# Two-layer block: the small parameters of a layer move from SyncE's load queue to GpSimd's, and two low halves take other places on VectorE

## The reference

```python
a = rms_norm(h, attn_norm[i])
proj = a @ w_in[i]                       # 1024 x 4632 columns, split below
(da_q, da_k, da_v, ssd_z, ssd_xbc, ssd_dt,
 gla_q, gla_k, gla_v, gla_g, gla_lr) = jnp.split(proj, IN_SPLITS, axis=-1)
y_da  = diff_attention(da_q, da_k, da_v, ...)   # q, k: rms_norm by head, gain, rope
y_ssd = ssd_mixer(ssd_z, ssd_xbc, ssd_dt, ...)  # xbc: 4-tap convolution, bias, silu
y_gla = gla_mixer(gla_q, gla_k, gla_v, gla_g, gla_lr, ...)
h = h + concat(y_da, y_ssd, y_gla) @ w_out[i]
f = rms_norm(h, ffn_norm[i])
h = h + (silu(f @ w_ffn_gate[i]) * (f @ w_ffn_up[i])) @ w_ffn_down[i]
h = h + sigmoid(h @ ple_w_gate[i]) * (p[i] @ ple_w_proj[i])
```

## Time and profile before

| | |
|---|---|
| median of 3 runs | 1769.35 us (1769.14 to 1770.1) |
| the profiled execution | 1768.65 us |
| its span in the trace | 1766.5 us |
| TensorE busy with matmuls | 1709.9 us, 97% of the span |
| VectorE busy | 1202.0 us, 68% |
| ScalarE busy | 908.3 us, 51% |
| GpSimd busy | 44.2 us, 3% |
| granted TensorE clock, mean | 0.997 of full speed |

### The profile page before, as it was taken

One profiled execution on the slowest core, in us unless ns is written; L12 is line 12 of the kernel. 1 busy time (PEld: TensorE's weight loads), 2 busy tenths in 40 slices (PEclk: granted clock), 3 DMA queues, 4 the chain that ended last, 5 costly groups with the idle time before them and its releaser, 6 DMA issues.

```text
span 1766.5 us, 33950 instructions
## 1 busy us (share of the span) xinstructions
PE 1709.9 (97%) x14158; PEld 1480.2 (84%) x14158; DVE 1202.0 (68%) x1673; ACT 908.3 (51%) x1122; POOL 44.2 (3%) x47
## 2 busy tenths in 40 slices
PE   7999999998999999999999999999999989999998
PEld 5877799986987789988978888888888868899896
DVE  5888765546678865545657768678677794577874
ACT  5565443335475443334554556445454563466772
POOL 2000000000000000000000000000000000000130
PEclk9999999999999999999999999999999999999999
DMA  7657568554557566655331322222222122352112
GB/s 198 192 191 288 165 169 193 183 196 160 150 179 269 206 162 184 190 191 180 86 91 59 92 73 73 73 73 85 73 61 85 61 97 96 114 175 64 48 65 103
DMA packets 252184, 238.18 MB, mean 135 GB/s; under 512 B 32816, under 2 KB 212064, under 8 KB 251776
## 3 DMA queue, kind: packets, MB, share of 16 engines
q1 hardware_dynamic: 250896, 233.21, 42.7%
q0 software_dynamic: 1136, 2.81, 0.7%
HBM read 234.94 MB, written 1.05 MB: 134 GB/s over the span
## 4 chain that ended last, share of the span: by engine, by line
PE 82%; DVE 6%; ACT 4%; DMA 3%; DVEq 2%; issue 1%; ACTq 1%; SPq 1%
PE pg L2629 35%; PE pg L1298 34%; PE pm L1298 8%; PE pm L2629 3%; PE pm L1301 2%; DMA ring<-in_ada_w 1%; DVE ring_r L572 1%; PE pm L2632 1%; DMA ring<-in_hg_w_in 1%; DMA ring<-in_w_in 1%; ACT ring_r L565 1%; DVE ring_r L1753 1%; SPq L2218 1%; DVEq L1789 1%; DMA cst<-in_cst 0%
## 5 line engine op out<-in xcount | busy, mean ns | idle before, releaser
L572 DVE TENSOR_TENSOR ring_r<-ring,ring_r 128x2048 fp32r<-128x2048 f32 (+1 forms) x126 | 283.7, 2260 | 157.1 <-ACT ring_r L565 151.3
L2629 PE MATMUL pg<-ring_r,work_r 128*128 128x512 f32 (+1 forms) x1632 | 377.9, 391 | 7.7 <-DVEq L3138 2.7
L2629 PEld LDWEIGHTS pg<-ring_r,work_r 128*128 128x128 f32 x1632 | 299.4, 189 | 76.6 <-issue 12.6
L1298 PE MATMUL pg<-ring_r,work_r 128*128 128x512 f32 (+3 forms) x1280 | 355.8, 383 | 2.7 <-DVE work_r L1759 1.4
L2629 PE MATMUL pg<-work_r,ring_r 128*128 128x256 f32 x2688 | 320.5, 282 | 6.9 <-DVE ring_r L572 3.8
L2629 PEld LDWEIGHTS pg<-work_r,ring_r 128*128 128x128 f32 x2688 | 318.9, 189 | 8.7 <-DVE ring_r L572 5.0
L565 ACT ACTIVATE ring_r<-ring 128x2048 fp32r<-128x2048 f32 (+1 forms) x126 | 237.1, 1889 | 169.9 <-DMA ring<-in_w_ffn_up 70.2
L1298 PE MATMUL pg<-ring_r 128*128 128x512 f32 (+3 forms) x752 | 284.3, 378 | 2.5 <-DVEq L823 1.3
L1298 PEld LDWEIGHTS pg<-ring_r,work_r 128*128 128x128 f32 x1280 | 235.5, 188 | 48.1 <-issue 2.9
L1298 PE MATMUL pg<-work_r,ring_r 128*128 128x512 f32 (+1 forms) x976 | 264.6, 361 | 0.0
L1298 PEld LDWEIGHTS pg<-work_r,ring_r 128*128 128x128 f32 x976 | 173.0, 189 | 27.3
(11 more groups left out here) (395 smaller groups left out, 1854.9 us busy)
## 6 DMA issues: line engine op xcount, KB each, us to landing
ring<-in_w_in SPq DMA_DIRECT2D x36, 1024.0 KB, 5.3
ring<-in_ada_w SPq DMA_DIRECT2D x24, 1024.0 KB, 6.9
ring<-in_hg_w_in SPq DMA_DIRECT2D x48, 512.0 KB, 3.8
ring<-in_w_ffn_gate SPq DMA_DIRECT2D x44, 512.0 KB, 4.0
ring<-in_w_ffn_up SPq DMA_DIRECT2D x44, 512.0 KB, 5.3
ring<-in_w_ffn_down SPq DMA_DIRECT2D x22, 1024.0 KB, 4.9
ring<-in_hg_w_in SPq DMA_DIRECT2D x64, 256.0 KB, 3.0
ring<-in_w_out SPq DMA_DIRECT2D x12, 1024.0 KB, 5.1
```

What stands on the lines that cost most here:

```text
L572: W.low_done(V.tensor_tensor(lo, W.raw(i, name)[:, 0:lo.shape[1]], W.hi(i, name).bitcast(f32), ALU.subtract))
L1298: return T.matmul(out_, lhsT, rhs, start=first, stop=last)
L2629: return T.matmul(out_, lhsT, rhs, start=first, stop=last)
```

## The change

The list `layer_parameters` and the loop `load_parameters` become functions that GpSimd uses. SP's queue then holds only `x`, the constants and weights; it no longer waits for `dak_1`. GpSimd issues the 22 loads of layer 0 behind its three first loads, then `p`, then the five vectors of the second block. It issues the 22 loads of layer 1 in one go, behind the memset that waits for `score2` of layer 0 and behind two new waits: the normed rows of the feed-forward part (`e_aT`, 8) and the fourth finished product of gate and up (`e_gu`, 4). On VectorE the low half of `small` moves ahead of the multiplication by the gain, and the low half of `gqk_0` moves between the ropes of tile 0 and tile 1, in both layers.

```diff
@@ sync
             load_w_in(0, w_in_pieces[1:4])
-            first_loads = layer_parameters(0)
-            W.wait_ready(sp, 0, "dak_1")
-            for k, (a, b) in enumerate(((0, 12), (12, 16), (16, N_PRM))):
-                load_parameters(first_loads[a:b])
-                load_w_in(0, w_in_pieces[4 + k:5 + k])
             for i in range(DEPTH):
-                load_w_in(i, w_in_pieces[4 if i else 7:])
+                load_w_in(i, w_in_pieces[4:])
...
-                    if next_loads and j == 6:
-                        e_aT.wait(sp, i, 8)
-                    if 6 <= j < 17:
-                        load_parameters(next_loads[2 * (j - 6):2 * (j - 5)])
@@ gpsimd
-            second_pool_early(pool)
+            load_parameters(pool, layer_parameters(0))
             for i in range(DEPTH):
...
                 pool.dma_start(q3(ptok, NT), d["p"][i, 0].rearrange("(t p) n -> p t n", p=P)).then_inc(loaded_p, 16)
+                if i == 0:
+                    second_pool_early(pool)
...
                 e_zero1.set(G.memset(Sz, 0.0))
+                if i + 1 < DEPTH:
+                    e_aT.wait(pool, i, 8)
+                    e_gu.wait(pool, i, 4)
+                    load_parameters(pool, layer_parameters(i + 1))
@@ vector
                 dve.drain()
+                low("small")
                 for t in range(NT):
                     V.tensor_tensor(qk5[:, t], qk5[:, t], bc(q3(p_qkg, 2), [2, HC, DQK], 2), ALU.mult)
                 dve.drain()
-                low("small")
                 for t in range(NT):
...
                     dve.drain()
+                    if t == 0:
+                        low("gqk_0")
                 e_qk.set(dve.drain())
-                low("gqk_0")
```

More of the change, by code:

```diff
@@ L2182, in second_dve, with layer_parameters, load_parameters @@
             V.tensor_tensor(h3[:, 1, half[1]], h3[:, 1, half[1]], rows_of(1, 1), ALU.add).then_inc(m_fin, 1)
+        def layer_parameters(i):
+            small_loads = [
+                (p_convb, cols("ssd_conv_b", i)),
+                (p_qkg[:, 0:DQK], rows("da_q_norm", i)), (p_qkg[:, DQK:], rows("da_k_norm", i)),
+                (p_bgate, cols("gla_b_gate", i)), (p_wg2[0:GLA_R, :], d["gla_w_gate2"][i]),
+                (p_dtb, rows("ssd_dt_bias", i)), (p_alog, rows("ssd_a_log", i)),
+                (p_lam[:, 0:64], rows("da_lambda_q1", i)), (p_lam[:, 64:128], rows("da_lambda_k1", i)),
+                (p_lam[:, 128:192], rows("da_lambda_q2", i)), (p_lam[:, 192:256], rows("da_lambda_k2", i)),
+                (p_dskip, rows("ssd_d", i)), (p_ssdn, rows("ssd_norm", i)), (p_glan[:, 0:1], cols("gla_norm", i)),
+                (p_sub[:, 0:1], cols("da_sub_norm", i)),
+                (p_ffn, cols("ffn_norm", i)), (p_li, d["lam"][i]),
+                (p_adab, d["ada_b_2"][i].rearrange("(c p) -> p c", p=P)),
+            ]
+            for j in range(4):
+                small_loads.insert(1 + j, (convw3[:, j, :], d["ssd_conv_w"][i, j].rearrange("(c p) -> p c", p=P)))
+            assert len(small_loads) == N_PRM
+            return small_loads
+        def load_parameters(eng, loads):
+            for dst, src in loads:
+                eng.dma_start(dst, src).then_inc(loaded_prm, 16)
         @block.sync
@@ L2196, in piece @@
                     W.loaded(sp.dma_start(dst(W.raw(i, name)), src), i, name)
-            def layer_parameters(i):
-                small_loads = [
-                    (p_convb, cols("ssd_conv_b", i)),
-                    (p_qkg[:, 0:DQK], rows("da_q_norm", i)), (p_qkg[:, DQK:], rows("da_k_norm", i)),
-                    (p_bgate, cols("gla_b_gate", i)), (p_wg2[0:GLA_R, :], d["gla_w_gate2"][i]),
-                    (p_dtb, rows("ssd_dt_bias", i)), (p_alog, rows("ssd_a_log", i)),
-                    (p_lam[:, 0:64], rows("da_lambda_q1", i)), (p_lam[:, 64:128], rows("da_lambda_k1", i)),
-                    (p_lam[:, 128:192], rows("da_lambda_q2", i)), (p_lam[:, 192:256], rows("da_lambda_k2", i)),
-                    (p_dskip, rows("ssd_d", i)), (p_ssdn, rows("ssd_norm", i)), (p_glan[:, 0:1], cols("gla_norm", i)),
-                    (p_sub[:, 0:1], cols("da_sub_norm", i)),
-                    (p_ffn, cols("ffn_norm", i)), (p_li, d["lam"][i]),
-                    (p_adab, d["ada_b_2"][i].rearrange("(c p) -> p c", p=P)),
-                ]
-                for j in range(4):
-                    small_loads.insert(1 + j, (convw3[:, j, :], d["ssd_conv_w"][i, j].rearrange("(c p) -> p c", p=P)))
-                assert len(small_loads) == N_PRM
-                return small_loads
-            def load_parameters(loads):
-                for dst, src in loads:
-                    sp.dma_start(dst, src).then_inc(loaded_prm, 16)
             whole8 = lambda s: s.rearrange("p (c n) -> p c n", c=KC)
@@ L2269, in _ @@
                 wu = d["w_ffn_up"][i].rearrange("(c p) n -> p c n", p=P)
-                next_loads = layer_parameters(i + 1) if i + 1 < DEPTH else []
                 for j, name in enumerate(gu_pieces):
```

## The result

| | before | after |
|---|---|---|
| median | 1769.15 us (1766.99 to 1770.1, 16 runs) | 1772.96 us (1771.38 to 1775.61, 16 runs) |
| span of the profiled execution | 1766.5 us | 1771.1 us |
| VectorE starts the low half of `xbc1_0` | 49.68 | 54.28 |
| the 16 transposes start | 82.64 | 88.89 |

A forecast was written before the change was run, and what follows sets the result against it. TensorE holds 82% of the chain, so time can only come from its gaps and slow stretches, here at layer 0's start. 1768.65 - 5.2 = 1763.4, with 0.7 for the median 1764.1 us; range 1762.8 to 1767.

The forecast's parts named there:

- landing of `xbc0_0`: Layer 0 start: this weight piece lands at 34.5 instead of 36.27, with no SP loads around it.
- VectorE starts `xbc1_0`: Layer 0: VectorE begins this low half at 44.55 instead of 49.68, 10.05 us after `xbc0_0` lands, set by ScalarE's chain.
- chain to the end of `gqk_1`: VectorE's work from the low half of `xbc1_0` through that of `gqk_1`: unchanged 27.14 us, ending at 71.7 instead of 76.82.
- wait ahead of the second half of `gqk`: TensorE in layer 0 wants the low half of `gqk_1` at 71.05, has it at 71.7: 0.65 us wait stays.
- GpSimd's 22nd load issued by: Layer 0's 22 loads on GpSimd start at 21.50, take 17.2 us, the last issued at 38.7.
- last of the 22 landed: Layer 0's small parameters all land by 43.2; VectorE waits for them at 46.8, margin 3.6 us.
- Theory 2: From the experiments, not the prediction: small loads of any other queue in flight beside a weight piece slow it.
- Theory 1: From the experiments, not the prediction: GpSimd's queue itself is the cause, its packets hold the DMA engines.
- rival A: Layer 0 start: only issue time is saved, `xbc0_0` lands at 36.27 as before; gain 3.5, 1765.9 us; chance 15%.
- The order: VectorE's earlier low halves of `small` and `gqk_0`: costed at 0, alone also about 0.
- C: Layer 0's parameters come late from GpSimd and move VectorE's chain; at 1.5 us a load 7 us slower, 1776; chance 8%.
- B: Behind 82 us or in layer 1: the shift is given back or not taken, 1767 to 1770 us; chance 12%.

The follow-up runs named there:

- seven first on SP: Kernel before with layer 0's seven early-needed small loads ahead of four weight pieces on SP, the other 15 behind, VectorE's order of before: 1762.41 us, ratio 0.9973.
- seven first, GpSimd: Changed kernel with GpSimd issuing seven early-needed loads first, then `p`, the 15 others and five vectors after `xbc1_1` landed: 1766.68 us, ratio 0.9999.
- ScalarE's queue: Kernel before with layer 0's 22 small loads issued by ScalarE instead of SP: 1774.19 us, ratio 1.0030.
- queues alone: Changed kernel with VectorE's order of before, so only the queues of the small loads are changed: 1771.95 us, ratio 1.0021.
- last six held: Changed kernel with GpSimd's last six loads (`p`, five vectors) held back until `xbc1_1` has landed: 1769.06 us, ratio 1.0010.
- order alone: Kernel before with only the new order of low halves on VectorE: 1769.98 us, ratio 1.0005.

## Why the prediction was wrong

Each forecast number beside what the changed kernel and, where the landing was undisturbed, the best version showed:

| step | forecast | after | seven first on SP |
|---|---|---|---|
| issues of `xbc0_0`, `xbc1_0` | 28.36, 33.9 | 28.28, 33.87 | 29.09 for the first |
| landing of `xbc0_0` | **34.5** (33.71 to 36.27) | **39.7** | 35.66 |
| VectorE starts `xbc1_0` | 44.55 | 54.28 | 45.81 |
| chain to the end of `gqk_1` | 27.14 | 27.24 | 27.16 |
| wait ahead of the second half of `gqk` | 0.65 | 1.79, then half clock | 1.21 |
| GpSimd's 22nd load issued by | 38.7 | 36.3 | |
| landing of `ada_b` after its issue | 4.5 | 10.3 | |
| last of the 22 landed | 43.2 | 45.2 | |
| the kernel | -5.2 us | +3.8 us | -5.1 us |

**The step that failed** is the landing: "both ends are bounds: landing at 33.71 or at 36.27", and I took 34.5 "because behind the change there is no SP load around it and the loads that GpSimd issues at that time are short rows". The upper end was no bound: the piece landed at 39.7. It was the row of a piece beside *some* small loads; the change put more of GpSimd's beside it, and for longer. That they were "short rows" was no reason for 34.5 either: the row loads of 32 KB took four times as much packet time in GpSimd's queue as in ScalarE's (below). The steps around it were right. In the best version, with its 0.73 us taken off, `xbc0_0` lands at 34.9, VectorE starts `xbc1_0` at 45.1 and the transposes start at 78.05: a gain of 4.6 us there where the sum said 5.2, the rest being the wait of 1.21 in place of 0.65. In the medians it is 5.1 us (3.0 to 6.7 by the interval).

**Why before was better than it looked.** Two queues shared the small loads. From 18 to 28 us, while no piece was in flight, they got 13 of the 28 through; the DMA view of that window, before:

```profile
q1 hardware_dynamic: 5902, 0.13, 36.0%
q0 software_dynamic: 224, 0.03, 19.6%
```

5902 packets of SP's queue, about half of its small ones, went while TensorE worked on pieces that had landed. GpSimd alone issues a load in 0.51 to 1.43 us, 28 of them in 19.8 us: the series reaches from 21.5 to 41.3 us, over `xbc0_0`, `xbc0_1` and `xbc1_0`. I had worked this out (the last of the 22 issued at 38.7) and asked only whether the parameters would be in time, not what they would do to the pieces.

**Theory 2 holds, with a remainder.** A different queue (ScalarE's) slows the pieces too, 38.26 and 43.93 where Theory 1 had at most 36.5 and 41.5; GpSimd's loads that fly later (the last six) cost 3 us less; and with GpSimd's queue empty from 29.7 us on `xbc0_0` lands at 35.2. In SP's own queue, 15 loads *behind* a piece cost it nothing (`xbc1_1`: 45.58 - 40.26 = 5.3 us, as undisturbed). The packets in the traces say how much company there was. While `xbc0_0` was between issue and landing, packets of the other queues, and small ones of SP's own, took this much time, summed over the 16 engines:

```
                          issue to landing   other queues   SP's own small
seven first, SP                6.58 us            0 us           0 us
seven first, GpSimd            6.69               7              0
before                         7.89              17             11
ScalarE's queue                9.22              26              0
after                         11.41              81              0
queues alone                  11.77              79              0
last six held                 12.27              85              0
```

From 6.6 to 11.4 are 4.8 us on each of 16 engines, 77 us, and GpSimd's packets took 81. It is an estimate, as packets overlap, and with ScalarE's queue it comes out less well (42 against 26). It also points at why GpSimd's loads cost more than ScalarE's. They did not take more in all: from 14 to 70 us ScalarE's queue took 135.5 us for the 22, GpSimd's 173.1 with its nine others, which alone took 48.3 in the run with ScalarE's queue, so about 125. But more of it fell beside the piece. Four of the six row loads of 32 KB landed there with GpSimd (35.2 to 37.6), with ScalarE only behind it (39.3 to 43.7), and the six took 52.8 us of packet time in GpSimd's queue and 13.2 in ScalarE's. How much of the lateness is due to the time of the loads and how much to the kind of queue isn't measured.

**The rule I had cited.** The Trainium skill (DMA: Bandwidth & Descriptors, "Issuing engines are not separate DMA queues") says that loads of several engines interleave on the same 16 DMA engines. The trace agrees: from 30 to 32 us the 16 engines started 23 packets of GpSimd's queue and 270 of SP's. The other half, that issuing from more engines only saves time on the sequencer, I took in rival A to mean a landing of 36.27 as before; measured 39.7. Interleaving is not neutral: a long transfer that shares each engine with another queue lands later than one that has it to itself.

**The order** was costed at 0, "alone it would also give about 0". Its effect on waits was right (the second half of `gqk` still starts at 76.9). I had not followed the clock: when alone, the wait that moved to a place between the halves took the stretch of 1.2 GHz with it, from a half with time to spare to the one on the path, 2.5 us in the transposes. With the queues the order made that wait 1.79 us instead of 1.53, and only behind the longer one did the clock fall. That is 1.2 us in the transposes (88.89 against 87.65), 1.8 when each is counted from the start of its q and k products (69.28 against 67.45). Where the pieces come in time it is free, 1762.54 against 1762.41.

**The rivals.** A had `xbc0_0` land at 36.27 as before; it landed at 39.7. C, the parameters too late, did not happen: they landed at 45.2, VectorE needed them at 56.6, and GpSimd issued the short rows in 0.51 to 0.57 us each. B's giving back in layer 1 did not happen either (next paragraph). None of the rivals had the loss in the pieces' landings.

**From 6.25 us at the transposes to 3.8 in the median.** The shift of TensorE against the kernel before (median over 11 matmuls of equal number, at a time of before):

```
                  83 us    853 us   1050 us  1200 us  1400 us  1760 us
after              6.26     6.53     6.15     5.66     4.54     4.58
queues alone       5.02     6.13     5.19     4.61     3.60     3.59
order alone        2.55     2.69     2.03     1.01     0.14     0.22
seven first       -3.85    -3.84    -4.52    -4.76    -5.05    -5.02
ScalarE's queue    5.84     5.80     5.49     5.58     5.56     5.64
```

Up to 853 us the shift stands to within 0.3 us, as forecast (with the queues alone it grows by 1.1). Then 1.2 to 2.5 us go, in the kernel that is ahead as in those that are behind, though not in that with ScalarE's queue. A part of it therefore need not be a giving back of this change; if the one profiled execution of before was slow there, it would look like this, but no run shows it. It stays open.

## What to carry to other kernels

Moving small loads off a busy queue is not free for the large ones: look at what will be in flight beside each large transfer on the path, and for how long, before asking whether the small ones arrive in time. Small loads did best in a stretch without a large one, or behind the last of a run of large ones in its own queue; put between two of them, they passed the delay on to the next. Give the few that are needed early their own semaphore and let the rest follow. And when a wait moves, look where the stretch of low clock behind it moves: covered by a later wait it cost nothing here (the first half of `gqk` before), and without one its full length (2.5 us with the order alone).

## What I had not expected of the hardware

One queue of small loads spreads the 16 engines of a 1 MB load from 2.1 us to 6.0 and 8.3 us (`xbc0_0` and `xbc0_1`), and their sum of bytes says nothing on it: 0.23 MB from GpSimd's queue had packets under way for 41.1% of the engines' time for ten microseconds. The packets of q0 and q1 in the trace, by size, in the changed kernel, with the mean time of one in ns (from 30 to 32 us, and 34 to 36 us):

```
30..32 us  q0: 4B: 8 x 9 ns    256B: 15 x 875 ns                    q1: 1024B: 270 x 68 ns
34..36 us  q0: 4B: 42 x 9 ns   256B: 8 x 44 ns   2048B: 35 x 641 ns q1: 1024B: 166 x 50 ns
48..50 us  q0: 4B: 1 x 9 ns                                         q1: 1024B: 664 x 52 ns
```

A packet isn't the same thing on the two kinds of queue. The six row loads of 32 KB (128 rows of 256 B each) are 96 packets of 2048 B on GpSimd's queue, 550 ns each in the mean, and 768 packets of 256 B on ScalarE's, 17 ns each: four times the packet time for the same rows. Loads by column go the other way: 1024 runs of 4 B are 16 packets of 256 B on GpSimd's queue (245 ns each from 21 to 28 us, when no piece was beside them) and 1024 packets of 9 ns on SP's. While GpSimd's packets ran, the weights passed 166 to 270 packets in 2 us instead of 664. Why they take so long, and whether the engine is busy or waits in that time, the trace doesn't say.
